# Forgetting attention: scores of long rows in two parts, and the masked rows, scalings and shares around them rearranged

## The reference

```python
for blk in range(t // 128):
    q0, q1 = blk * 128, blk * 128 + 128
    s = jnp.einsum('bqhd,bkhd->bhqk', q[:, q0:q1], k[:, :q1]) * ATTN_SCALE
    s = s + c_h[:, :, q0:q1, None] - c_h[:, :, None, :q1]
    s = jnp.where(arange(q1)[None, :] <= (q0 + arange(128))[:, None], s, NEG_INF)
    p = softmax(s)
    outs.append(einsum('bhqk,bkhd->bqhd', p, v[:, :q1]))
main = concatenate(outs) * sigmoid(gate)
```

## Time and profile before

| what | us |
|---|---|
| median of 3 runs | 2978.84 |
| lowest and highest of them | 2965.72, 2980.3 |
| span of the profiled execution, first to last instruction | 2974.8 |
| of it the forgetting attention, 1948 to 2166 | 218 |
| one pair of heads in it, in the steady part | 34.76 |

### The profile page before, as it was taken

How to read it: one execution, slowest core, us unless ns; L and a number is a source line. 1 busy time by engine, 2 the same in 40 slices (tenths; PEclk the granted TensorE clock), 3 DMA queues, 4 the chain that set the end, 5 groups by cost and what they waited for, 6 DMA issues and landing times. The chain is left out here.

```text
span 2974.8 us, 56716 instructions
## 1 busy us (share of the span) xinstructions
PE 2791.2 (94%) x23069; PEld 2243.1 (75%) x23069; DVE 1870.3 (63%) x2527; ACT 1201.8 (40%) x2178; POOL 1305.4 (44%) x1112
## 2 busy tenths in 40 slices
PE   7999989999799999998999999988889999999998
PEld 5888777777667788887887777756667788887787
DVE  6333566666443756556986788867752865556895
ACT  3111343333233433334444766545542433334442
POOL 6344234444232545456554454422112555556653
PEclk9999899999799999999999999999999999999999
DMA  5333100010031233336543232342122233335651
GB/s 199 107 100 105 59 25 24 25 46 4 24 127 65 78 128 113 114 114 205 161 123 93 57 100 89 109 164 86 65 78 86 77 119 106 110 114 174 191 142 68
DMA packets 290602, 295.37 MB, mean 99 GB/s; under 512 B 11623, under 2 KB 223709, under 8 KB 289193
## 3 DMA queue, kind: packets, MB, share of 16 engines
q1 hardware_dynamic: 288440, 286.89, 30.6%
q10 hardware_dynamic: 1424, 4.83, 0.4%
q0 software_dynamic: 480, 0.03, 0.0%
HBM read 200.30 MB, written 88.65 MB: 97 GB/s over the span
## 5 line engine op out<-in xcount | busy, mean ns | idle before, releaser
L312 POOL TENSOR_TENSOR w_lo_b<-w_raw_b,w_hi_b 128x512 fp32r<-128x512 f32 (+3 forms) x540 | 748.0, 1388 | 672.8 <-ACT w_hi_b L346 669.5
L396 PE MATMUL ps<-b_hi,w_hi_b 128*128 128x512 f32 x1540 | 610.4, 396 | 9.2 <-issue 9.2
L396 PE MATMUL ps<-b_lo,w_hi_b 128*128 128x512 f32 x1540 | 602.7, 391 | 0.0
L396 PE MATMUL ps<-b_hi,w_lo_b 128*128 128x512 f32 x1540 | 602.3, 391 | 0.0
L346 ACT ACTIVATE w_hi_b<-w_raw_b 128x512 fp32r<-128x512 f32 (+3 forms) x498 | 295.2, 596 | 454.9 <-PE ps L3370 198.1
L396 PEld LDWEIGHTS ps<-b_hi,w_hi_b 128*128 128x128 f32 x1540 | 291.4, 189 | 74.7 <-issue 14.2
L396 PEld LDWEIGHTS ps<-b_lo,w_hi_b 128*128 128x128 f32 x1540 | 291.4, 189 | 63.9 <-issue 3.9
L396 PEld LDWEIGHTS ps<-b_hi,w_lo_b 128*128 128x128 f32 x1540 | 291.1, 189 | 61.1
L3370 PE MATMUL ps<-b_hi,w_hi_b 128*128 128x512 f32 x616 | 245.9, 399 | 24.3 <-DVE x_res L3187 23.8
L3370 PE MATMUL ps<-b_lo,w_hi_b 128*128 128x512 f32 x616 | 242.6, 394 | 0.0
L3370 PE MATMUL ps<-b_hi,w_lo_b 128*128 128x512 f32 x616 | 242.5, 394 | 0.0
(11 more groups left out here) (429 smaller groups left out, 5786.6 us busy)
## 6 DMA issues: line engine op xcount, KB each, us to landing
w_raw_b<-in_w_gate_up SPq DMA_DIRECT2D x88, 512.0 KB, 4.3
act_dram<-x_res SPq DMA_DIRECT2D x44, 512.0 KB, 6.1
sum_dram<-x_res SPq DMA_DIRECT2D x40, 512.0 KB, 2.9
w_raw_b<-in_w_down SPq DMA_DIRECT2D x28, 512.0 KB, 5.8
stage<-sum_dram SPq DMA_DIRECT2D x54, 256.0 KB, 3.8
stage<-act_dram SPq DMA_DIRECT2D x50, 256.0 KB, 4.2
w_raw_a<-in_a_w_in SPq DMA_DIRECT2D x23, 512.0 KB, 4.7
u_dram<-evac_a SPq DMA_DIRECT2D x16, 512.0 KB, 3.0
```

The source lines that it names most:

```text
L312: nc.gpsimd.tensor_tensor(self.wlo[:, r, 0:n, :], source, self.whi[:, r, 0:n, :].bitcast(F32), ALU.subtract).then_inc(self.w_lo, 1)
L396: mm = self.nc.tensor.matmul(self.ps[:, bank, :], w[:, r, k, :], h[:, block, k, :], start=(start and k == 0 and a == 0 and h is self.bh), ...
```

## The change

It concerns `phase_fox` alone.

- Scores of a wide unit are made in two parts, of 512 columns and of the rest. Parts are numbered over all units and take turns between two banks for each head; a part waits only for the reduction of the part two before it, and each part has its own signal to DVE.
- DVE reduces a part with one instruction. The last part of each unit (for short units the only one) takes its decay from `decay_masked`, which POOL now makes for each unit and head over the whole last part (128 to 512 columns) by adding a row `future` that is 384 zeros and then the mask. There are three such buffers; POOL waits for the unit three before.
- DVE copies `by_dve` tiles of a wide unit (4, 3, 2, 2 for t = 7, 6, 5, 4) in place of 4, ACT the rest.
- The outputs of four units lie in bank 6 in falling order of place, so that each scaling is one instruction of 512 columns in place of four.
- The reciprocals move ahead of the copy of head 0, the spreading on PE moves to the next round behind `values`, and the gate scaling moves from the head of a round to behind the reduction of head 1.

```diff
+            future = sb("future", [P, HALF])
-            decay_masked = sb("decay_masked", [P, 2, 2, T])
+            decay_masked = sb("decay_masked", [P, 3, 2, HALF])
...
+            by_dve = lambda n: {7: 4, 6: 3, 5: 2, 4: 2}[units[n][1]]
+            parts = [(n, a) for n in range(N) for a in range(2 if wide(n) else 1)]
+            part_at = {x: i for i, x in enumerate(parts)}
+            last_part = lambda n: 1 if wide(n) else 0
+            part_keys = lambda n, a: (a * HALF, min((units[n][1] + 1) * P, (a + 1) * HALF))
+            part_bank = lambda n, a, h: ps[:, 2 * h + part_at[n, a] % 2, 0:part_keys(n, a)[1] - part_keys(n, a)[0]]
...
+            place = lambda n: 3 - n % 4
...
             @block.gpsimd
-                for p in range(PAIRS):
-                    rest_wait(pool, p)
-                    if p >= 2:
-                        pool.wait_ge(lowest, 2 * TT * (p - 1))
-                    for _, t in units[TT * p:TT * (p + 1)]:
-                        at = slice(t * P, (t + 1) * P)
-                        for h in range(2):
-                            nc.gpsimd.tensor_tensor(decay_masked[:, p % 2, h, at], decay[p % 2][:, h, at], future, ALU.add).then_inc(masked, 1)
+                nc.gpsimd.memset(future[:, 0:HALF - P], 0.0)
+                link(nc.gpsimd.tensor_copy(future[:, HALF - P:HALF], self.const("future")))
+                for n, (p, t) in enumerate(units):
+                    if n % TT == 0:
+                        rest_wait(pool, p)
+                    lo, hi = part_keys(n, last_part(n))
+                    for h in range(2):
+                        if n >= 3:
+                            pool.wait_ge(reduced, reductions[n - 3, h, last_part(n - 3)])
+                        nc.gpsimd.tensor_tensor(decay_masked[:, n % 3, h, 0:hi - lo], decay[p % 2][:, h, lo:hi],
+                                                future[:, HALF - (hi - lo):HALF], ALU.add).then_inc(masked, 1)
...
                 def scores(n):
-                    pe.wait_ge(lowest, 2 * n)
-                    for c in range(0, nk, HALF):
-                        w = min(HALF, nk - c)
+                    for a in range(last_part(n) + 1):
+                        lo, hi = part_keys(n, a)
+                        if part_at[n, a] >= 2:
+                            m, c = parts[part_at[n, a] - 2]
+                            pe.wait_ge(reduced, reductions[m, 1, c])
                         for h in range(2):
-                            mm = mmul(ps[:, 2 * h + c // HALF, 0:w], ...)
-                    mm.then_inc(scored, 1)
+                            mm = mmul(part_bank(n, a, h), ...)
+                        mm.then_inc(scored, 1)
...
                     if i >= 2:
                         values(i - 2)
+                        if i % 4 == 1:
+                            spread_shares(i // 4 - 1)
                     if 1 <= i <= N:
                         turn(i - 1, 1)
-                        if i % 4 == 0:
-                            spread_shares(i // 4 - 1)
...
             @block.vector
+                def reduce(n, h):
+                    p, t = units[n]
+                    if n % TT == 0 and h == 0:
+                        rest_wait(dve, p)
+                    for a in range(last_part(n) + 1):
+                        lo, hi = part_keys(n, a)
+                        last = a == last_part(n)
+                        dve.wait_ge(scored, part_at[n, a] + 1)
+                        if a == 0 and h == 0 and n >= 2:
+                            dve.wait_ge(turned_d, turns(n - 1))
+                            dve.wait_ge(turned_a, turns(n - 1))
+                        if last:
+                            dve.wait_ge(masked, 2 * n + h + 1)
+                        if a:
+                            dve.wait_ge(reduced, reductions[n, h, 0])
+                        nc.vector.tensor_tensor_reduce(
+                            out=prob[:, n % 2, h, lo:hi], in0=part_bank(n, a, h),
+                            in1=decay_masked[:, n % 3, h, 0:hi - lo] if last else decay[p % 2][:, h, lo:hi], scale=1.0,
+                            scalar=least[:, n % 2, h, 0:1] if a else 3e38, op0=ALU.add, op1=ALU.min,
+                            accum_out=least[:, n % 2, h, 1:2] if last else least[:, n % 2, h, 0:1]).then_inc(reduced, 1)
...
+                for i in range(N + 2):
+                    if i < N:
+                        reduce(i, 0)
+                    if ends_four(i - 1):
+                        ...
+                        nc.vector.reciprocal(share[:, n // 4 % 2, :], total[:, n // 4 % 2, :]).then_inc(shared, 1)
+                    if 1 <= i <= N:
+                        turned_copy(i - 1, 0)
+                    if i < N:
+                        reduce(i, 1)
+                    if ends_four(i - 2):
+                        dve.wait_ge(spread, n // 4 + 1)
+                        nc.vector.tensor_tensor(as_tiles(scale[:, n // 4 % 2, :]), as_tiles(ps[:, 7, :]), four_tiles(gate[p % 2], n), ALU.mult).then_inc(scaled, 1)
+                    if 1 <= i <= N:
+                        turned_copy(i - 1, 1)
+                    if ends_four(i - 2):
+                        dve.wait_ge(summed, n // 4 + 1)
+                        dve.wait_ge(scaled, n // 4 + 1)
+                        nc.vector.tensor_tensor(four_tiles(self.X[:, p, :], n), as_tiles(ps[:, 6, :]), as_tiles(scale[:, n // 4 % 2, :]), ALU.mult).then_inc(stored, 1)
```

More of the change, by code:

```diff
@@ L2379, in phase_fox @@
             turns = lambda n: sum(2 if wide(m) else 1 for m in range(n))
+            by_dve = lambda n: {7: 4, 6: 3, 5: 2, 4: 2}[units[n][1]]
[4 more added lines that the diff above has]
+            part_bank = lambda n, a, h: ps[:, 2 * h + part_at[n, a] % 2, 0:part_keys(n, a)[1] - part_keys(n, a)[0]]
+            reductions = {x: i + 1 for i, x in enumerate((n, h, a) for n in range(N) for h in range(2) for a in range(2 if wide(n) else 1))}
+            place = lambda n: 3 - n % 4
+            four_tiles = lambda x, n: x.rearrange("p (b s c) -> p s b c", b=2, c=P)[:, 2 * (1 - n // 4 % 2):2 * (1 - n // 4 % 2) + 2]
+            as_tiles = lambda x: x.rearrange("p (s b c) -> p s b c", b=2, c=P)
             def rest_wait(engine, p):
@@ L2444, in values @@
                         for h in range(2):
[L2445 removed]
+                            mm = mmul(ps[hs[h], 6, place(n) * P:(place(n) + 1) * P], v[b][:, j, hs[h]], prob_t[:, n % 2, h, j, :], start=(j == 0), stop=(j == t))
                     if n % 4 == 3:
@@ L2452, in turn @@
                     if wide(n):
+                        d = by_dve(n)
                         pe.wait_ge(copied_d, turns(n) + h)
-                        for j in range(4):
+                        for j in range(d):
                             mm = nc.tensor.transpose(ps[:, 4, j * P:(j + 1) * P], prob[:, n % 2, h, j * P:(j + 1) * P], self.const("ident"))
@@ L2518, in _ @@
             def _(dve):
-                link = self.linker(dve, self.vector_link)
                 flat = lambda x: x.rearrange("p a c -> p (a c)")
[L2521 to L2527, removed]
-                            last = nc.vector.tensor_tensor(scale[:, n // 4 % 2, m * P:(m + 1) * P], ps[:, 7, m * P:(m + 1) * P],
-                                                           gate[p % 2][:, units[n - 3 + m][1] * P:(units[n - 3 + m][1] + 1) * P], ALU.mult)
-                        last.then_inc(scaled, 1)
-                    n = i
-                    if n < N:
-                        p, t = units[n]
-                        nk = (t + 1) * P
-                        dve.wait_ge(masked, 2 * (n + 1))
-                        dve.wait_ge(scored, n + 1)
-                        if n >= 2:
+                def reduce(n, h):
[7 more added lines that the diff above has]
+                        if a == 0 and h == 0 and n >= 2:
@@ new lines, in turned_copy @@
+                def turned_copy(m, h):
+                    tm = units[m][1]
+                    if wide(m):
+                        d = by_dve(m)
+                        dve.wait_ge(turned_d, turns(m) + h + 1)
+                        nc.vector.tensor_copy(flat(prob_t[:, m % 2, h, 0:d, :]), ps[:, 4, 0:d * P]).then_inc(copied_d, 1)
+                    elif h == 0:
+                        dve.wait_ge(turned_d, turns(m) + 1)
+                        nc.vector.tensor_copy(flat(prob_t[:, m % 2, h, 0:tm + 1, :]), ps[:, 4, 0:(tm + 1) * P]).then_inc(copied_d, 1)
```

56 lines of the change are left out of this document (17 added, 39 removed).

## The result

In five runs each the changed kernel took 2951.03 us in the median (2944.25 to 2957.63), the kernel before 2968.58 (2965.72 to 2980.3; the 2978.84 ahead of the prediction was the median of its first three). The medians differ by 17.6 us. The ratio on record is not that of the two medians (0.9941) but 0.9921, 95% interval 0.9901 to 0.9942; taken of 2968.58 it means about 23.5 us less, between 17 and 29. The forecast was 20.1 us less, and 2958.7 counted from the earlier median. The times of the whole program can't tell 20.1 from 24 us; what the forecast had wrong is seen in the phase alone. PE's waits did go and the time fell, but the new period and the first pair were priced too small, and the price of each single edit was wrong.

The account below looks back on a forecast made before the run. PE's own work was taken as the bound, its waits as winnable: 17.2 us in five pairs, 2.9 in the first, 0 at the end, 20.1 off 2974.8, so 2954.7 us (2958.7 from the median); range 2946 to 2970.

Parts of the forecast that it names:

- the new period, 31.13 + 0.2: Steady pair of the attention phase: PE's busy 31.13 us plus 0.2 us of remaining wait, 31.3 in place of 34.76.
- the six brackets: Six idle places in PE's timeline of a steady pair before the change, 3.59 us in all, the most winnable.
- The rival that named this: PE's batch records overlap their successors, so true idle is longer: period 30.7 to 30.9, gain 24 us, 2955; chance 0.08.
- First pair 2.9: First pair of the phase: earlier DVE start and four later waits save 2.9 us, bounds 1.5 and 3.6.
- The waits, one by one: PE's idle by cause: 2.16 us for reciprocals before the spreading, 0.64 for copies of bank 4, 0.79 for scores.
- The wait at t = 3 of 0.2: PE's scores of t = 3 still wait about 0.2 us for the first part of head 1's reduction.
- A gap between two parts: New wait and signal between a wide unit's two score parts: nearly 0, at most 0.18 us each, 0.7 for the range.
- The end, 0: End of the phase, up to the next phase's first matmul: no change, bounds 1 us either way.
- DVE 21.1, ACT 18.9, POOL 14.6: Predicted busy us in a pair: DVE down by 3.9, ACT up from 17.84, POOL up from 6.65.
- Shutting out: DVE's and POOL's additions cannot run side by side: 6 us slower, 2985, up to 15 us, 2994; chance 0.05.
- A wait that stays: New waits in PE's in-order loop leave 1.5 us idle each period, losing 9 of 20 us: 2968; chance 0.20.
- The rule of the Trainium skill: Weight loads fill 21.03 of 34.76 us, so PE could be fed up to DVE's 21.1: 80 us saved, 2898; chance 0.02.

Follow-up runs that it names:

- Order alone: Kernel before, with only the spreading behind the next round's values, reciprocals ahead of head 0's copy, gate scaling behind head 1: pair 33.78 us.
- in one piece: Changed kernel, with PE waiting until the whole unit before is reduced and DVE waiting for all scores of a unit: pair 34.38 us.
- the same copy: Changed kernel, spreading by four transposes from a broadcast copy of the reciprocals: copy on DVE, pair 30.33 us; on POOL, 29.65 us.

## Where the prediction was right, and which step failed

The step that failed is the new period, 31.13 + 0.2: PE's busy time was taken for its work, and the six brackets for all of its waiting. That gave 3.43 us for each pair, and the runs show 4.18. Beneath it the split by cause failed too: the spreading's waits were priced at 2.16 us for the new order, and alone it is worth 0.98. That the medians of the whole program give 17.6 us, near the 20.1 of the forecast, is luck: the median of before fell by 10.3 us once it had five runs.

The phase's gain of 24.85 us splits into 4.05 for the first pair, 4 x 4.18 and 4.08 for the last pair and the end. Step by step:

- **PE's own work is the bound and the waits are what can be won: right**, shown by the spreading done twice and by the masks and DVE's work that could be added almost without cost.
- **New period 31.3: too long by 0.72, the first mis-sized term, 3.6 of 4.75 us missed.** I took PE's busy 31.13 as its work and the brackets, 3.59, as its idle time. A record overlaps its successor by 0.07 us (1.99 against 1.92 from start to start), so each batch ahead of a wait carries 0.07 too much. By distances of starts, equal batches subtracted, PE waited 1.72 + 0.53 + 0.43 + 0.58 + 0.09 + 0.50 + 0.24 = 4.09 us, with one wait, 0.09, that has no bracket. The rest is that a spreading between values and a turn is cheaper than between a turn and scores, 0.14 twice: 34.76 - 4.09 - 0.28 + 0.16 = 30.55. The rival that named this had a chance of 0.08, and its 30.7 to 30.9 was still too long, for it had the overlap but not the place of the spreading.
- **First pair 2.9: 4.05 in the two profiled executions, above its bounds of 1.5 to 3.6, the second term, 1.15 us.** The start went as walked: DVE began at 1956.29, 1.68 us after PE, not 3.94, and PE's first wait was 1.46 and not 3.11 us. The first wait gave back 1.65 us for the 1.4 priced; the later waits and the spreading's place were again undervalued, by distances as in a steady pair they are worth about 2.1 us for the 1.48 priced. What is left, about 0.3 us, can't be told from the clock, by which a first pair came out up to 1.7 us shorter against its steady pair (0.78 for 2.50 us). So that the term was too small is sure of the later waits; that it lies outside the bounds rests on one execution of each kernel.
- **The waits, one by one: the sum right, the assignment wrong.** I gave 2.16 us to the reciprocals' order and 0.79 to the parts. Order alone is worth 0.98, and in one piece the rest of the change is worth 0.38 us for each pair (0.60 less than the order alone, as DVE pays for the cut at 512). The two waits for DVE at t = 7 coincide, and a bracket names only the one that stands first.
- **The wait at t = 3 of 0.2: 0.16. A gap between two parts, nearly 0 on PE:** the eight records of a wide unit still take 1.99 us. On DVE the same step is not nothing: its two reductions of a wide head were to take "the same 1.44 us", and the distance between them grew by 0.15 us, hidden here by DVE's room. **The end, 0: it grew by 0.10** (36.59 less a pair of 30.58, against 40.67 less 34.76); there PE's last values wait 0.52 us for ACT's copy, one of the signs named, but only this once.
- **DVE 21.1, ACT 18.9, POOL 14.6: 21.39, 18.81, 13.73.** Their savings count little, as said.
- **The rivals.** Shutting out did not happen in the changed kernel. A wait that stays did not either, but for the 0.16. The rule of the Trainium skill (Perfetto Trace Analysis, Identifying the Most-Contended Engine), by which weight loads (with the share of peak arithmetic) and not matmul busy time tell how near PE is to its limit, would have left PE headroom: loads fill 21.07 of 30.58 us. The doubled spreading found none at its two places: it added 1.75 us of loads and 1.75 us to the pair. What lies in the gaps between loads was not tried.

## What to carry to other kernels

Where an in-order engine is the bound, add up the distances from start to start of its equal batches, and call what exceeds them waiting; busy time with modelled ends hides some of it. Before a wait gets a price of its own, ask what would stop the engine next at the same place: two waits that end on the same event must be removed together, and either alone looks nearly worthless. Once the engine is shown to be the bound by giving it more work, give it less, and put the work that replaces it on an engine where it holds up nothing that the bound engine waits for: the same copy gave 0.25 us for each pair on DVE and 0.93 on POOL.

## What the runs showed of the hardware

PE's clock fell after waits of under 2 us. With the order alone, two pairs look alike in their waits, 1.60 us each, but in one of them the granted clock was 0.57 of full speed over the four us that follow, and the pair took 35.40 us in place of 33.78:

```profile
2014.70:2018.70 4.00, 4.00 (x42) 3.22 (x42) 3.68 (x15) 2.06 (x7) 0.00 (x0) 1.00 0.02 4
2048.50:2052.50 4.00, 4.00 (x31) 3.46 (x30) 2.36 (x9) 1.47 (x5) 0.00 (x0) 0.57 0.00 0
```

Between 2049 and 2052 it stood at 0.50, the lower of its two levels (1.2 of 2.4 GHz); PE had been at work again since 2047.46.

The kernel in one piece, with 1.88 us at that place, had two such pairs of four (35.96 against 34.38). The kernel before waited 1.65 us in each pair ahead of the spreading and had none in its steady pairs. What decides is open.

GpSimd's additions cost less for each column in wide instructions: 455 ns for 128 columns, 1275 for 512.
